# Second layer's attention in 32 pairs of heads, with a new order of the start and of the shared-key stage

## The reference

```python
def swa_mixer(h, w_in, sinks, k_sh, v_sh, cos, sin):
    q, mq = jnp.split(h @ w_in, [SWA_Q_W], axis=-1)          # 12 query heads of 64, 4 memory heads of 64
    q = apply_rope(q.reshape(B_, S_, SWA_Q_HEADS, HEAD_DIM), cos, sin)
    return swa_sink_attention(q, k_sh, v_sh, sinks), mq       # 4 kv heads, window 128, a sink logit per head
...
    s = jnp.where(valid, einsum(q, kband) * (dh ** -0.5), -inf)   # 128 queries against 256 keys
    m = jnp.maximum(jnp.max(s, axis=-1, keepdims=True), sink)
    p = jnp.exp(s - m)
    p = p / (jnp.sum(p, axis=-1, keepdims=True) + jnp.exp(sink - m))
    o = jnp.einsum('bnhgqk,bnkhd->bnqhgd', p, vband)
...
        mix = jnp.concatenate([main, memory_attention(mq, mk, mv)], axis=-1) @ w_out[l]
        x = x + rmsnorm(mix, g_mix_post[l])
```

## Time and profile before

| | |
|---|---|
| median of 3 runs | 2105.72 us (2099.66 to 2108.97) |
| the profiled execution | 2103.98 us, of which the profile's span is 2102.5 |
| mean granted TensorE clock | 0.990 of full |
| TensorE busy | 2017.2 us, 96% |
| VectorE, ScalarE, GpSimd busy | 1178.0, 930.2, 243.1 us |
| chain that ended last | TensorE 81%, VectorE 11%, ScalarE 6% |

### The profile page before, as it was taken

One profiled execution on the slowest core, in us unless ns is written; L12 is line 12 of the kernel. 1 busy time (PEld: TensorE's weight loads), 2 busy tenths in 40 slices (PEclk: granted clock), 3 DMA queues, 4 the chain that ended last, 5 costly groups with the idle time before them and its releaser, 6 DMA issues.

```text
span 2102.5 us, 25443 instructions
## 1 busy us (share of the span) xinstructions
PE 2017.2 (96%) x10048; PEld 1673.8 (80%) x10048; DVE 1178.0 (56%) x2592; ACT 930.2 (44%) x1907; POOL 243.1 (12%) x194
## 2 busy tenths in 40 slices
PE   7999999999999899999999999999999999999998
PEld 7987788887887777788887888878767887877786
DVE  5426454443226677464443126998976627867744
ACT  6447454443124467454443123367744233256630
POOL 1001010000001000010000002576730300000001
PEclk9999999999999999999999999999999999999999
DMA  6321122222223122222222223222222222210131
GB/s 234 117 84 41 61 90 91 91 99 100 100 100 130 60 71 101 91 91 101 88 93 101 100 100 103 98 81 81 81 94 96 100 81 80 101 41 21 41 120 60
DMA packets 28087, 190.07 MB, mean 90 GB/s; under 512 B 3184, under 2 KB 3328, under 8 KB 6720
## 3 DMA queue, kind: packets, MB, share of 16 engines
q1 hardware_dynamic: 24848, 175.98, 24.4%
q0 software_dynamic: 2544, 10.37, 1.5%
q10 hardware_dynamic: 576, 2.10, 0.2%
HBM read 184.24 MB, written 4.19 MB: 90 GB/s over the span
## 4 chain that ended last, share of the span: by engine, by line
PE 81%; DVE 11%; ACT 6%; issue 1%; POOL 1%; DMA 0%; SPq 0%; DVEq 0%; ACTq 0%; POOLq 0%
PE bank L427 23%; PE bank L428 23%; PE bank L429 23%; DVE bank L2178 4%; PE bank L1851 2%; PE bank L1839 1%; PE bank L575 1%; PE bank L1233 1%; DVE WL L394 1%; ACT WH L373 1%; PE bank L1844 1%; PE bank L1737 1%; DVE WL L399 1%; PE bank L1218 1%; ACT WH L370 1%
## 5 line engine op out<-in xcount | busy, mean ns | idle before, releaser
L427 PE MATMUL bank<-XH,WH 128*128 128x512 f32 (+2 forms) x1536 | 598.1, 389 | 14.8 <-DVE XL L591 6.1
L429 PE MATMUL bank<-XH,WL 128*128 128x512 f32 (+2 forms) x1536 | 569.9, 371 | 0.0
L428 PE MATMUL bank<-XL,WH 128*128 128x512 f32 (+2 forms) x1536 | 569.5, 371 | 0.0
L427 PEld LDWEIGHTS bank<-XH,WH 128*128 128x128 f32 (+1 forms) x1536 | 289.1, 188 | 76.3 <-issue 14.2
L428 PEld LDWEIGHTS bank<-XL,WH 128*128 128x128 f32 (+1 forms) x1536 | 289.3, 188 | 53.2 <-issue 6.0
L429 PEld LDWEIGHTS bank<-XH,WL 128*128 128x128 f32 (+1 forms) x1536 | 288.9, 188 | 50.1
L399 DVE TENSOR_TENSOR WL<-RAW,WH 128x2048 fp32r<-128x2048 f32 x64 | 146.7, 2292 | 309.8 <-ACT WH L373 309.8
L373 ACT ACTIVATE WH<-RAW 128x2048 fp32r<-128x2048 f32 x86 | 164.4, 1911 | 277.6 <-PE bank L429 277.6
L394 DVE SCALAR_TENSOR_TENSOR WL<-RAW,cols,WH 128x256 fp32r<-128x256 f32 (+2 forms) x424 | 188.5, 515 | 75.7 <-ACT WH L370 75.6
L370 ACT ACTIVATE WH<-RAW,cols 128x256 fp32r<-128x256 f32 (+2 forms) x424 | 187.6, 524 | 39.0 <-PE bank L429 39.0
L2178 DVE SCALAR_TENSOR_TENSOR bank<-conv_in,cols,bank 128x512 f32<-128x512 f32 x290 | 198.1, 747 | 1.1
(11 more groups left out here) (323 smaller groups left out, 3060.3 us busy)
## 6 DMA issues: line engine op xcount, KB each, us to landing
RAW<-weights SPq DMA_DIRECT2D x164, 1024.0 KB, 4.8
row_a<-rows POOLq DMA_DIRECT2D x6, 512.0 KB, 6.0
x_res<-x SPq DMA_DIRECT2D x1, 2048.0 KB, 15.8
kv<-mem_park POOLq DMA_DIRECT2D x2, 1024.0 KB, 5.1
out<-x_res ACTq DMA_DIRECT2D x4, 512.0 KB, 2.6
mem_tok<-mem SPq DMA_DIRECT2D x1, 1024.0 KB, 4.9
mem_tok<-mem POOLq DMA_DIRECT2D x1, 1024.0 KB, 5.3
mem_park<-m_keys POOLq DMA_DIRECT2D x2, 512.0 KB, 2.9
```

Source lines behind the costliest of these rows:

```text
L427: pe.matmul(ps, ah, bh, start=first, stop=False)
L428: pe.matmul(ps, ah, bl, start=False, stop=False)
L429: return pe.matmul(ps, al, bh, start=False, stop=last)
```

## The change

The attention of layer 1 runs over 32 pairs of jobs instead of 64 single ones. Scores of a pair lie side by side in one buffer, are scaled by VectorE with the reciprocal before they are turned, and are turned into one PSUM bank and copied at once. The values are now the weights of the product (64 columns each) and `T` moves; the two heads write the lower and the upper 64 partitions of one bank. So the output arrives turned, and ScalarE and VectorE write its high and low part (`mixed_high`, `XL`) directly. `turn_mixed` is gone, and three of the four tiles of the first half of the output product are made in the last steps of the attention. The lags of the woven splits are 1 and 2 steps of a pair.

In the shared-key stage the statistics of the second memory come first in VectorE's queue and take one root for both tiles, its load is issued before the late roots, and the keys are rotated two tiles at a time between the low parts.

At the start, the constants are loaded in two pieces, x in four; the first projection's units 0 to 3 come before the four memory units; the first memory is loaded ahead of unit 4, scaled after the gates and the rotation tables, turned once (16 transposes) and multiplied after the projection's second chunk; its gains are applied to the weights.

```diff
-    order = run(("mem_kv", 0), 2) + run(("mem_kv", 1), 2)
-    order += run("in_a", 12) + run(("out", 0), 4) + run(("ffn_in", 0), 22) + run(("ffn_out", 0), 12)
+    order = run("in_a", 4) + run(("mem_kv", 0), 2) + run(("mem_kv", 1), 2) + run("in_a", 12)[4:]
+    order += run(("out", 0), 4) + run(("ffn_in", 0), 22) + run(("ffn_out", 0), 12)
...
+            if u == 4:
+                sp.dma_start(mem_tok[0][:, :, :], mem_in[0].rearrange("(t p) d -> p t d", p=P)).then_inc(
+                    *mem_there.mark("mem", by=16))
...
+        def load_x(half, pair):
+            there = x_there[half, pair].mark("x", half, pair, by=16)
+            s = slice(512 * half, 512 * half + 512)
+            sp.dma_start(x_res[:, 2 * pair:2 * pair + 2, s],
+                         x_in[0].rearrange("(t p) d -> p t d", p=P)[:, 2 * pair:2 * pair + 2, s]).then_inc(*there)
+        sp.dma_start(const[:, 0:K_BLOCK], const_in[:, 0:K_BLOCK]).then_inc(*loaded_first.mark(by=16))
+        sp.dma_start(cols[:, GC_MIXPRE[0]:N_COLS], cols_in[:, GC_MIXPRE[0]:N_COLS]).then_inc(*loaded_first.mark("first", by=16))
         for j in range(2):
             sp.dma_start(RAW[j][:, :], weights_in[j]).then_inc(*raw[j].mark("unit", j, by=16))
-        sp.dma_start(x_res[:, :, :], x_in[0].rearrange("(t p) d -> p t d", p=P)).then_inc(*x_there.mark("x", by=16))
+            for pair in range(2):
+                load_x(j, pair)
+        sp.dma_start(const[:, K_BLOCK:K_END_1], const_in[:, K_BLOCK:K_END_1]).then_inc(*loaded.mark(by=16))
+        sp.dma_start(cols[:, 0:GC_MIXPRE[0]], cols_in[:, 0:GC_MIXPRE[0]]).then_inc(*loaded.mark(by=16))
+        sp.dma_start(pos[:, :], pos_in).then_inc(*loaded.mark("constants", by=16))
...
     def in_a_pe():
+        PE.wait_ge(*after("first"))
+        first_tiles_pe(0, 0)
+        first_product_pe(0, 0)
+        first_tiles_pe(0, 1)
+        for t in (1, 2):
+            first_product_pe(t, 0)
+        first_tiles_pe(1, 0)
+        first_product_pe(3, 0)
+        first_tiles_pe(1, 1)
         for t in range(NT):
-            PE.wait_ge(*after("emptied", "n0", t, 1))
-            chunk_tile_pe(U["in_a", 0], ("in_a", 0), t, 0, A_CHUNK, KB, from_x, last=t == NT - 1)
-        in_a_unit_pe(0, 1)
+            first_product_pe(t, 1)
         in_a_unit_pe(1, 0)
-        in_a_unit_pe(1, 1)
+        PE.wait_ge("split_lo", U["in_a", 3] + 1)
+        for t in range(NT):
+            chunk_tile_pe(U["in_a", 3], ("in_a", 1), t, 4, A_CHUNK, KB, from_x, last=t == NT - 1)
+            if t == 1:
+                turn_memory_pe()
...
     def in_b_dve():
-        chunk_out_dve(units=2)
-        rotate_dve(kv_tok, SKV, ("kv",), 0, "k")
+        memory2_stats_dve()
+        for first in range(0, NT, 2):
+            lower_dve()
+            rotate_dve(kv_tok, SKV, ("kv",), 0, "k", range(first, first + 2))
         memory2_dve()
-        chunk_out_dve()
+        lower_dve()
...
     def feed_forward_pool(layer):
...
+        if layer == 0:
+            load_memory2_pool()
+            late_roots_pool(("n2", 0))
...
+            step = [(stage, n - lag) for stage, lag in ((2, VALUE_LAG), (1, TURN_LAG), (0, 0)) if 0 <= n - lag < PAIRS]
             other = beside(n)
             for stream, k in woven(len(step), len(other)):
                 if stream == 1:
                     beside_pe(other[k])
                     continue
-                stage, i = step[k]
+                stage, p = step[k]
                 if stage == 0:
-                    slide_scores_pe(i)
-                    slide_scores_pe(i + 1)
-                elif i < 16:
-                    memory_job_pe(stage, i, i, 1, None, "six")
-                elif stage == 2:
-                    PE.wait_ge(*after("swa_recip", i - 16))
-                    turn_scores_pe(("swa", i - 16), S_of(i, SEQ, 1), band(SWA[i - 16][0]), "six")
-                elif stage == 3:
-                    t, h = SWA[i - 16]
-                    PE.wait_ge(*after("emptied", "turn", "swa", i - 16))
-                    ps = take_bank("six", "swa_out", i - 16)
-                    n_keys = band(t) // P
-                    for c in range(n_keys):
-                        mm = pe.matmul(ps[:, 0:HD], T_of(i, SEQ, 1)[:, c * P:(c + 1) * P],
-                                       kv_tok[:, t - n_keys + 1 + c, 256 + h // 3 * HD:256 + (h // 3 + 1) * HD],
-                                       start=c == 0, stop=c == n_keys - 1)
-                    mm.then_inc(*T.mark("full", "swa_out", i - 16))
+                    slide_scores_pe(2 * p)
+                    slide_scores_pe(2 * p + 1)
+                elif stage == 1:
+                    slide_turn_pe(p)
+                else:
+                    slide_values_pe(p)
+            if n >= PAIRS and n < PAIRS + 3:
+                out_tile_pe(n - PAIRS, 0)
...
+    def slide_turn_pe(p):
+        PE.wait_ge(*after("slide_scaled", p))
+        ps = take_bank("six", "slide_turn", p)
+        for c in range(2 * slide_width(p) // P):
+            mm = pe.transpose(ps[:, c * P:(c + 1) * P], S_buf[p % 4][:, c * P:(c + 1) * P], ident)
+        mm.then_inc(*T.mark("full", "slide_turn", p))
+    def slide_values_pe(p):
+        PE.wait_ge(*after("emptied", "slide_turn", p))
+        ps = take_bank("six", "slide_out", p)
+        n = slide_width(p) // P
+        for c in range(n):
+            for i in range(2):
+                mm = pe.matmul(ps[HD * i:HD * i + HD, 0:P], slide_value(2 * p + i, c),
+                               T_buf[p % 4][:, (n * i + c) * P:(n * i + c + 1) * P], start=c == 0, stop=c == n - 1)
+                if c == n - 1:
+                    mm.then_inc(*(T.mark("full", "slide_out", p) if i else T.mark()))
...
+    def slide_exp_act(p):
+        ACT.wait_ge(*after("slide_max", p))
+        if p < 8 and p >= 4:
+            ACT.wait_ge(*after("full", "slide_turn", p - 4))
+        for i in range(2 * p, 2 * p + 2):
+            S = slide_scores_of(i)
+            if p < 8:
+                act.activation(S, bank_of("mem", 1, i)[:, 0:MEM], AF.Exp, bias=stat(1, i), scale=HD ** -0.5,
+                               accum_out=stat(2, i)).then_inc(*A.mark("emptied", "mem", 1, i))
+            else:
+                act.activation(S, S, AF.Exp, bias=stat(1, i), accum_out=stat(2, i)).then_inc(*A.mark())
+        if p >= 8:
+            act.activation(stat_pair(3, p), stat_pair(3, p), AF.Exp).then_inc(*A.mark("slide_exp", p))
...
+            if 0 <= n - PART_LAG < PAIRS:
+                slide_high_act(n - PART_LAG)
+            if 0 <= n - TURN_LAG < PAIRS:
+                slide_turn_act(n - TURN_LAG)
+            if n < PAIRS:
+                slide_exp_act(n)
...
+    def slide_scaled_dve(p):
+        if p < 8:
+            DVE.wait_ge(*after("emptied", "mem", 1, 2 * p + 1))
+        else:
+            DVE.wait_ge(*after("slide_exp", p))
+            dve.tensor_tensor(stat_pair(2, p), stat_pair(2, p), stat_pair(3, p), ALU.add).then_inc(*V.mark())
+            DVE.wait_ge(*V.so_far())
+        dve.reciprocal(stat_pair(4, p), stat_pair(2, p)).then_inc(*V.mark())
+        DVE.wait_ge(*V.so_far())
+        for i in range(2 * p, 2 * p + 2):
+            S = slide_scores_of(i)
+            dve.tensor_scalar(S, S, stat(4, i), None, ALU.mult).then_inc(*(V.mark("slide_scaled", p) if i % 2 else V.mark()))
+    def slide_low_dve(p):
+        kb, tt = pair_place(p)
+        DVE.wait_ge(*after("high", "slide_out", p))
+        dve.tensor_tensor(XL[:, kb, tt], bank_of("slide_out", p)[:, 0:P], mixed_high[:, kb, tt].bitcast(F32),
+                          ALU.subtract).then_inc(*V.mark("emptied", "slide_out", p))
...
     def out_first_pe(layer):
         if layer:
-            turn_mixed_pe(layer, ready)
-            PE.wait_ge(*after("emptied", "mixed", layer, KB - 1))
-            chunk_pe(U["out", layer, 0], ("out", layer, 0), 512, KB, NT, from_x)
+            out_tile_pe(3, 0)
+            for t in range(NT):
+                out_tile_pe(t, 1)
```

More of the change, by code:

```diff
@@ L200, in build @@
     parked_keys, parked_values = tally("parked_keys"), tally("parked_values")
-    mem_there, mem2_there, x_there = tally("mem_there"), tally("mem2_there"), tally("x_there")
+    mem_there, mem2_there, loaded_first = tally("mem_there"), tally("mem2_there"), tally("loaded_first")
+    x_there = {(half, pair): tally(f"x_there_{half}_{pair}") for half in range(2) for pair in range(2)}
     in_row_a, in_row_b = tally("in_row_a"), tally("in_row_b")
@@ L270, in build @@
     mixed = place("mixed", [P, NT, D], offset=big + 61568)
+    m1_parts = [place(f"m1_{part}", [P, KB, MEM], F32R, offset=big + o) for part, o in (("high", 65536), ("low", 73728))]
+    mixed_high = place("mixed_high", [P, KB, SEQ], F32R, offset=big + 61568)
     mqT = place("mqT", [P, 2, SEQ], offset=big + 77952)
@@ L493, in from_x, with from_mixed @@
         return XH, XL, kb
+    def from_mixed(kb):
+        return mixed_high, XL, kb
     def from_y(kb):
@@ L718, in tail_pool, with late_roots_pool @@
```

(48 more changed lines are left out.)

314 lines of the change are left out of this document (146 added, 168 removed).

## The result

The change made the kernel slower. Four runs of it have a median of 2126.46 us (2125.24 to 2127.8), four of the kernel before 2104.07; the ratio is 1.0105, with a 95% interval of 1.0086 to 1.0124. The prediction was 2080, with 2071 to 2097 as its range, and gave "slower" a chance of 0.04. The profiled execution took 2127.8 us, its span is 2126.3.

A forecast was written before the change was run, and what follows sets the result against it. TensorE, busy in 96% of the span, was taken as the bound. Gains of 6 at the start, 7 in the projections and 12.5 in the attention, 25.5 in all, took 2105.7 to 2080 us; range 2071 to 2097.

The forecast's parts named there:

- Part 1: Start of the kernel: first product at about 10.3 us instead of 18.39; gain 6, bounds 2 and 8.
- the 1.7 MB at 249 GB/s: Start: data the first product needs, at the earlier mean load rate, 6.8 us, taken as 8 with the landing.
- Part 2: Key and query projections: TensorE's 5.0 us wait for the scaled second memory goes, with its after-effects; gain 7, bounds 4 and 8.
- Part 3: Attention with the turning behind it: five terms together gain 12.5 us, or 2.8 with column halves one after the other.
- (a): End of the attention: the turning of the mixed rows goes, 32 transposes and their waits; gain 7.0 us.
- (c): Last three attention steps: each gets a tile of the output product where TensorE had only short jobs; gain 1.5 us.
- (d): Attention's value products: two heads side by side in column halves, 0.29 us a visit for the mode change; gain 5.0.
- (e): Attention's pace: VectorE and ScalarE's chain 3.4 us a pair, about equal to TensorE's need; 4 us charged for missed beats.
- (b): Attention: the unit's split goes in quarters, later, so most of TensorE's waits at the first scores go; gain 3 us.
- The rival that ended slower: Attention: VectorE paces the pairs, its whole queue uncovered by the exponents, 4.35 us a pair; chance 0.03.

The follow-up runs named there:

- Parts 1 and 2 alone: Changed kernel with its attention and the output product behind it put back as before, only start and projections changed: 2093.82 us, ratio 0.9951.
- the run with the split first: Changed kernel with high and low parts moved in their queues, plus split quarters on ScalarE ahead of the exponents and VectorE's lower quarter one step earlier: 2079.09 us.
- with the quarters close: Quarters at four entries in a row: on the changed kernel 2115.56 us, on that with high and low parts moved 2097.72; which is meant isn't said.

## Why the prediction was wrong, point by point

**Part 1, the start.** Forecast: first product at 10.3, gain 6. The product came at 13.65 in the profile after, and the gates' first log sums, behind the memory, at 81.72 instead of 85.06, 3.3 earlier (2.8 to 4.1 in the other profiles with this start). ScalarE got unit 0 at
```profile
9.67 2.28 ACT L379 ACTIVATE WH<-RAW,cols 128x428 fp32r<-128x428 f32 x4 [7.44 <-DMA RAW<-weights]
```
where I had it near 6. The term that failed is the 1.7 MB at 249 GB/s: the rate was that of a load order with a megabyte of memory at its head, where the new one has small pieces beside the first of unit 0. Of the 3.35 us by which the product was late, some 2 are the small rows (13.23 against 11.17); where the rest comes from stays open.

**Part 2, the projections.** Forecast 7; from the turn of k to the first scores the changed kernel gained 6.2 (684.17 to 732.49 before, 685.78 to 727.93 after). The scaling ended 2.8 before TensorE asked for it at 686.65, where 2.9 was forecast (VectorE, timeline after):
```profile
682.32 1.53 DVE L890 TENSOR_SCALAR mem_tok<-mem_tok,small 128x1024 f32<-128x1024 f32 x2
```
What remains is a wait of 1.4 for ScalarE's k (chain of work after):
```profile
686.04 2.56 ACT WH L379 x4
688.60 0.49 ACT kT L1603
...
689.13 1.14 PE bank L804 x8
```
Parts 1 and 2 alone are 11.3 by the medians, 13 was forecast. Right within their bounds. One profile alone can't tell it: in the nine with this start and these projections the first scores are 4.6 to 10.5 earlier than in the kernel before.

**Part 3.** (a) and (c), the turning gone and the steps at the end filled, are right: the last value product starts at 890.0 and the turn at 927.11 follows 37.1 later, 48.7 before. Two tiles of the output product went ahead of it, 24 products at 0.23 or 5.5 of these 11.6; 6.1 are the turning, forecast at 7.0. The 1.5 of (c) isn't shown by itself. (d) is right: eight products at the array's halves and the change there and back take 0.69, from 790.95 to 791.76 less the 0.12 of a plain product. By the forecast's terms such a pair is 4 x 0.11 + 0.29 = 0.73.

(e) is the step that failed, with (b)'s "in quarters, later". I took 3.4 us for VectorE's maxima, ScalarE's exponents and VectorE's scaling in a row, compared it with TensorE's 3.6 less 0.16 and charged 4 us for missed beats. That loop is really 3.33, as the run with the split first shows. But it isn't the only loop. A second one runs through the ring of banks: scores, maxima, exponents, quarters, high part, low part, scores, 4.74 us. I had priced the low part as 0.2 us of VectorE's time and never asked what is queued ahead of its high part on ScalarE, nor who waits for the bank. And I never asked at which step TensorE needs the last quarter. Together they put some 31 us of waits and 17 of clock into a stretch forecast at 157.1: it took 199.2. Put right, it takes 152.2, and the whole kernel 2079.09 with the start as it was: the forecast of 2080 is the time of this change with another order in two queues. That the two agree within 1 us is in part luck: the stretch gained 17.4 there where 12.5 was forecast, and start and projections 11.3 where 13 was.

The rival that ended slower had the right size, 4.35 a pair against 4.74, and the wrong cause. It let VectorE's whole queue go uncovered; in fact VectorE was idle in four tenths of the time and waiting for ScalarE. The argument against it, that the quarter stands behind the maxima under the exponents, is true in the trace (809.69) and says nothing on the loop that decided. Its chance of 0.03 was far too small for a sum that left 0.04 us a pair between TensorE's need and this loop, and that counted only one of the two loops.

Open: how the 47 us divide between the two causes where they overlap, and whether the quarters' edge comes from the move ahead of the exponents or from VectorE's lag; those two were changed together.

## What to carry to other kernels

When steps of a software pipeline grow, recount every lag in microseconds and list every loop that closes through a buffer ring, not only the one through the data: for each bank, who takes it next, which instruction frees it, and what stands ahead of that instruction on each engine it needs. Work that has slack goes into an engine's idle time, ahead of the instruction for which the engine waits, and not behind it where another queue depends on what follows. A short evacuation at the end of a long queue costs that whole queue.

## What the hardware showed that was not expected

The same instructions fall to the low clock in one execution and not in another. Windows of three kernels whose instructions up to here are those of the start before or after, first before, then after, then with the quarters close:
```profile
205.00:215.00 10.00, 8.55 (x50) 6.54 (x49) 8.60 (x28) 7.23 (x21) 1.96 (x4) 1.00 0.01 2
```
```profile
205.00:215.00 10.00, 8.55 (x40) 6.45 (x39) 8.12 (x29) 6.16 (x19) 2.00 (x4) 0.83 0.32 106
```
```profile
205.00:215.00 10.00, 8.88 (x46) 6.18 (x46) 8.48 (x32) 6.52 (x18) 1.89 (x3) 1.00 0.31 107
```
The second and third run the same program up to here, half a microsecond apart. Through three such stretches, near 208, 232 and 525, the changed kernel's profile gave back 4.9 us of its lead between the log sums and the turn of k, and the third, at the full clock in all three, kept it. What decides it is not shown. Two series of one kernel stood 4.5 us apart in their medians (0.2%), so a gain of 2 us at the start was shown by the trace alone.

One 10 KB load in 32 packets made the first product some 2 us later (10.98 to 11.25 without it ahead, 12.67 to 13.75 with it).

Two products in the array's column halves start within 0.02 us of each other, whether the heads are issued in turn or one after the other. The Trainium skill (TensorEngine Tiling (Array Packing), Key Properties) has different tiles of the array work in parallel; the runs agree, with these 0.02 us, for column halves.
